# Where the two halves of each split operand lie in SBUF: tensor homes on 512-byte steps, and high and low half of a held operand side by side

## What is computed

```python
for layer in range(2):
    h = rms_norm(x, g_mix[layer])
    qkv = h @ w_in[layer]                    # 1024 x 3072
    ...                                      # attention gives mix
    x = x + mix @ w_out[layer]               # 1024 x 1024
    h2 = rms_norm(x, g_ffn[layer])
    u = h2 @ w_up[layer]                     # 1024 x 5632, then the convolution
    gate, val = jnp.split(u, 2, axis=-1)
    x = x + (jax.nn.silu(gate) * val) @ w_down[layer]   # 2816 x 1024
...                                          # second block: branches, w_out_2
q = h @ peer_wq                              # 1024 x 2048
hid = gelu(h @ peer_u.T)                     # 1024 x 16384, all experts
x = x + (gates * hid) @ peer_v               # 16384 x 1024
```

## Time and profile before

| | |
|---|---|
| median of 3 runs | 1750.53 us (1750.17 to 1751.01) |
| the profiled execution, its span | 1747.2 us |
| around the span, median less span | 3.3 us |
| TensorE busy, weight loads | 1691.7 us (97%), 1454.8 us (83%) |
| VectorE, ScalarE, GpSimd busy | 1149.2 us, 821.6 us, 706.5 us |
| HBM traffic | 279.33 MB read, 161 GB/s over the span |

### The profile page before, as it was taken

How to read it: one execution, slowest core, us unless ns; L and a number is a source line. 1 busy time by engine, 2 the same in 40 slices (tenths; PEclk the granted TensorE clock), 3 DMA queues, 4 the chain that set the end, 5 groups by cost and what they waited for, 6 DMA issues and landing times.

```text
span 1747.2 us, 27224 instructions
## 1 busy us (share of the span) xinstructions
PE 1691.7 (97%) x10714; PEld 1454.8 (83%) x10714; DVE 1149.2 (66%) x2422; ACT 821.6 (47%) x1453; POOL 706.5 (40%) x384
## 2 busy tenths in 40 slices
PE   7999999999999998999999999999999999999997
PEld 6779998777799986544579999999999988888885
DVE  6655785756367576666332999999999644444443
ACT  5455665354476642113243554544444455555553
POOL 2424667132357721432163999700000144444443
PEclk9999999999999999999999999999999999999998
DMA  7333545463255564323353656544444566666664
GB/s 292 112 109 132 182 162 195 150 217 108 74 193 190 173 203 134 111 87 109 95 194 134 216 167 198 179 147 145 145 140 139 160 193 193 194 194 195 195 193 134
DMA packets 77455, 283.20 MB, mean 162 GB/s; under 512 B 8720, under 2 KB 8976, under 8 KB 77072
## 3 DMA queue, kind: packets, MB, share of 16 engines
q1 hardware_dynamic: 76032, 276.50, 48.8%
q10 hardware_dynamic: 1296, 4.97, 0.8%
HBM read 279.33 MB, written 2.10 MB: 161 GB/s over the span
## 4 chain that ended last, share of the span: by engine, by line
PE 78%; DVE 8%; ACT 5%; POOL 5%; issue 3%; DMA 1%; POOLq 0%; DVEq 0%; ACTq 0%
PE bank L542 62%; PE bank L533 7%; PE bank L597 5%; POOL wl L2117 4%; ACT wh L1112 2%; DVE att L1478 2%; PE bank L665 1%; DVE wl L1461 1%; ACT att L1115 1%; PE bank L967 1%; PE bank L889 1%; DVE ssb L1467 1%; DVE mix L1506 1%; DVE xs L1467 1%; PE bank L837 0%
## 5 line engine op out<-in xcount | busy, mean ns | idle before, releaser
L2117 POOL TENSOR_TENSOR wl<-raw,wh 128x1024 fp32r<-128x1024 f32 x213 | 548.0, 2584 | 699.6 <-ACT wh L1112 691.1
L542 PE MATMUL bank<-hh,wh 128*128 128x256 f32 x1856 | 526.2, 284 | 5.5 <-POOL wl L2117 4.8
L1112 ACT ACTIVATE wh<-raw 128x1024 fp32r<-128x1024 f32 x476 | 492.7, 1050 | 57.2 <-PE bank L542 40.8
L542 PE MATMUL bank<-hl,wh 128*128 128x256 f32 x1856 | 519.1, 280 | 0.0
L542 PE MATMUL bank<-hh,wl 128*128 128x256 f32 x1856 | 518.1, 279 | 0.0
L1461 DVE TENSOR_TENSOR wl<-raw,wh 128x1024 fp32r<-128x1024 f32 x263 | 352.8, 1347 | 98.7 <-ACT wh L1112 98.2
L542 PEld LDWEIGHTS bank<-hh,wh 128*128 128x128 f32 x1856 | 349.1, 188 | 7.0 <-POOL wl L2117 6.0
L542 PEld LDWEIGHTS bank<-hl,wh 128*128 128x128 f32 x1856 | 349.2, 188 | 0.0
L542 PEld LDWEIGHTS bank<-hh,wl 128*128 128x128 f32 x1856 | 349.0, 188 | 0.0
L1467 DVE TENSOR_TENSOR acl<-H,ach 128x256 fp32r<-128x256 f32 x128 | 87.5, 685 | 181.6 <-ACT ach L1115 181.6
L542 PE MATMUL bank<-wh,ach 128*128 128x512 f32 x512 | 199.3, 389 | 0.4 <-DVE acl L1467 0.4
(11 more groups left out here) (216 smaller groups left out, 2313.4 us busy)
## 6 DMA issues: line engine op xcount, KB each, us to landing
raw<-in_ut_dram SPq DMA_DIRECT2D x128, 512.0 KB, 3.5
raw<-in_vt_dram SPq DMA_DIRECT2D x128, 512.0 KB, 3.8
raw<-in_wup_dram SPq DMA_DIRECT2D x88, 512.0 KB, 4.2
raw<-in_win_dram SPq DMA_DIRECT2D x48, 512.0 KB, 4.6
raw<-in_wdown_dram SPq DMA_DIRECT2D x44, 512.0 KB, 4.2
raw<-in_wout_dram SPq DMA_DIRECT2D x24, 512.0 KB, 3.6
raw<-in_wga_dram SPq DMA_DIRECT2D x16, 512.0 KB, 3.6
raw<-in_wpq_dram SPq DMA_DIRECT2D x16, 512.0 KB, 5.1
```

What stands on the lines that cost most here:

```text
L542: m = p.e.matmul(out, lhs[i][a], rhs[i][b], start=start and i == 0 and j == 0, stop=stop and i == n - 1 and j == 2)
L1112: a.e.activation(high_of(u), raw_of(u), ACTF.Copy).then_inc(act_hi.up(("hi", u)), 1)
L2117: g.e.tensor_tensor(low_of(u), raw_of(u), high_of(u).bitcast(F32), ALU.subtract).then_inc(pool_lo.up(("lo", u)), 1)
```

## The change

All tensors get sizes that are multiples of 128 floats (512 bytes) and `pad0` in front of them sets the first of them on such a step, so that every operand starts at a multiple of 512 bytes (a scratch of the DMA queues that the kernel does not use is made smaller to make room). High and low half of one operand now share one tensor. Where the operand is **held** by TensorE, each element's high half and low half lie side by side, so a half is read with a step of two floats (8 bytes): weights of `wup`, `wpq`, `ut` (`turned_units`), the activations `hT_held`, `y2`, `ac2`. Where it **moves**, the high half and then the low half lie as two contiguous blocks, as before. The engines that write a half, and those that read it to make the low half, do so with the same step. The number, order, shapes and engines of all instructions stay, and so do all waits.

```diff
+        scoped(ctx, "pad0", 96)
         xs = scoped(ctx, "xs", 2048)
...
-        hh, hl = scoped(sc_h, "hh", 2048, F32R), scoped(sc_h, "hl", 2048, F32R)
+        h2 = scoped(sc_h, "h2", 4096, F32R)
...
-        sta = scoped(ctx, "sta", 760)
+        sta = scoped(ctx, "sta", 768)
         raws = [scoped(ctx, f"raw{i}", 1024) for i in range(4)]
-        whs = [scoped(ctx, f"wh{i}", 1024, F32R) for i in range(4)]
-        wls = [scoped(ctx, f"wl{i}", 1024, F32R) for i in range(4)]
+        w2s = [scoped(ctx, f"w{i}", 2048, F32R) for i in range(4)]
...
-        con_s = scoped(early, "con", K_W - 128)
-        sml_s = scoped(early, "sml", S_W)
+        con_s = scoped(early, "con", 1664)
+        sml_s = scoped(early, "sml", 896)
...
-        yTh, yTl = [scoped(sc_f, f"y{c}", NTILE * 256, F32R)[:, :].rearrange("p (k t) -> p k t", k=NTILE) for c in "hl"]
+        y2 = scoped(sc_f, "y2", 2 * NTILE * 256, F32R)[:, :].rearrange("p (k t a) -> p a k t", k=NTILE, a=2)
+        yTh, yTl = y2[:, 0], y2[:, 1]
...
-        ach = [scoped(ctx, f"ach{j}", 256, F32R)[:, :] for j in range(2)]
-        acl = [scoped(ctx, f"acl{j}", 256, F32R)[:, :] for j in range(2)]
+        ac2 = [scoped(ctx, f"ac{j}", 512, F32R)[:, :].rearrange("p (t a) -> p a t", a=2) for j in range(2)]
+        ach, acl = [a[:, 0] for a in ac2], [a[:, 1] for a in ac2]
...
+        turned_units = set(itertools.chain(*[range(first["wup", L], first["wup", L] + 2 * NTILE) for L in range(DEPTH)],
+                                           range(first["wpq"], first["wpq"] + 16), range(first["ut"], first["ut"] + 128)))
+
+        def halves(i):
+            return w2s[slot[i]][:, :].rearrange("p (c a) -> p a c", a=2) if i in turned_units else w2s[slot[i]][:, :].rearrange("p (a c) -> p a c", a=2)
+
         def high_of(i):
-            return whs[slot[i]][:, 0:plan[i][1]]
+            return halves(i)[:, 0, 0:plan[i][1]]
 
         def low_of(i):
-            return wls[slot[i]][:, 0:plan[i][1]]
+            return halves(i)[:, 1, 0:plan[i][1]]
...
-        hTh = hh[:, :].rearrange("p (k t) -> p k t", k=8)
-        hTl = hl[:, :].rearrange("p (k t) -> p k t", k=8)
+        hT_moving = h2[:, :].rearrange("p (a k t) -> p a k t", a=2, k=8)
+        hT_held = h2[:, :].rearrange("p (k t a) -> p a k t", k=8, a=2)
...
+        def halves_for(st):
+            return hT_moving if st[0] == "f" else hT_held
...
-    nc = _bacc.Bacc("TRN2", target_bir_lowering=False, num_devices=1)
+    nc = _bacc.Bacc("TRN2", target_bir_lowering=False, num_devices=1, dynamic_dma_scratch_size=1024)
```

More of the change, by code:

```diff
@@ L1 @@
+import itertools
 import math
@@ L106, in program @@
         sc_h = ExitStack()
-        hh, hl = scoped(sc_h, "hh", 2048, F32R), scoped(sc_h, "hl", 2048, F32R)
+        h2 = scoped(sc_h, "h2", 4096, F32R)
         sc_h.close()
         hw, sel_s = scoped(ctx, "hw", 2048), scoped(ctx, "sel_s", 2048)
-        sta = scoped(ctx, "sta", 760)
+        sta = scoped(ctx, "sta", 768)
         raws = [scoped(ctx, f"raw{i}", 1024) for i in range(4)]
-        whs = [scoped(ctx, f"wh{i}", 1024, F32R) for i in range(4)]
-        wls = [scoped(ctx, f"wl{i}", 1024, F32R) for i in range(4)]
+        w2s = [scoped(ctx, f"w{i}", 2048, F32R) for i in range(4)]
         early = ExitStack()
-        con_s = scoped(early, "con", K_W - 128)
-        sml_s = scoped(early, "sml", S_W)
+        con_s = scoped(early, "con", 1664)
+        sml_s = scoped(early, "sml", 896)
         tab_s = scoped(early, "tab", 8192)
         raws += [scoped(early, f"raw{i}", 1024) for i in (4, 5)]
-        whs += [scoped(early, f"wh{i}", 1024, F32R) for i in (4, 5)]
-        wls += [scoped(early, f"wl{i}", 1024, F32R) for i in (4, 5)]
+        w2s += [scoped(early, f"w{i}", 2048, F32R) for i in (4, 5)]
         sc_l = ExitStack()
@@ L303, in sml, with hT @@
             return sml_s[:, c:c + n]
-        def hT(k, cols):
-            return hTh[:, k, cols], hTl[:, k, cols]
+        def halves_for(st):
+            return hT_moving if st[0] == "f" else hT_held
+        def hT(k, cols, of=hT_held):
+            return of[:, 0, k, cols], of[:, 1, k, cols]
         iota = con(K_IOTA, 128)
@@ L436, in program @@
         H = H_s[:, :].rearrange("p (j t) -> p j t", j=128)
-        R_AT = 16800
-        assert R_AT >= K_W - 128 + S_W + 8192 + 6144
+        R_AT = 16896
+        assert R_AT >= 1664 + 896 + 8192 + 6144
         r_at = [R_AT]
@@ L616, in by_features @@
                             m = mm3(banks[b][:, 0:256], [unit_pair(i, k, kt, tcols(c)) for k in range(kt)],
-                                    [hT(off + k, ALLC) for k in range(kt)], True, True, ready)
+                                    [hT(off + k, ALLC, hT_moving) for k in range(kt)], True, True, ready)
                         else:
@@ L798, in pe @@
                         m = mm3(banks[b][:, 256 * half:256 * half + 256], [unit_pair(i, k, 8, tcols(0)) for k in range(8)],
-                                [hT(k, ALLC) for k in range(8)], True, True, ready_both(("f", L)))
+                                [hT(k, ALLC, hT_moving) for k in range(8)], True, True, ready_both(("f", L)))
                         m.then_inc(pe_out.up(("used", i), ("up", L, f, half)), 1)
@@ L1040, in hidden @@
                 claim(b)
-                m = mm3(banks[b][:, 0:256], [unit_pair(i, k, 8, tcols(0)) for k in range(8)], [hT(k, ALLC) for k in range(8)], True, True, ready_both(("f", 2)))
+                m = mm3(banks[b][:, 0:256], [unit_pair(i, k, 8, tcols(0)) for k in range(8)], [hT(k, ALLC, hT_moving) for k in range(8)], True, True, ready_both(("f", 2)))
                 m.then_inc(pe_out.up(("used", i), ("hid", j)), 1)
@@ L1141, in turned @@
                         a.wait_ge(pe_out, ("T", st, t, k))
-                        do(hTh[:, k:k + n, tcols(t)], quad(ps("T", st, t, k), n), ACTF.Copy, ("hTh", st, t, k))
+                        do(halves_for(st)[:, 0, k:k + n, tcols(t)], quad(ps("T", st, t, k), n), ACTF.Copy, ("hTh", st, t, k))
             def exps(tag, maps, buf, i):
@@ L1163, in act @@
             stream_up_to(first["win", 0])
-            load(con_s[:, :], consts_d[:, 128:K_W], con_in, "con")
+            load(con_s[:, 0:K_W - 128], consts_d[:, 128:K_W], con_in, "con")
             load(sml(0, S_W), smalls_d, sml_in, "sml")
@@ L1178, in out_turned @@
                     a.wait_ge(pe_out, ("mT", L, g))
-                    do(hTh[:, 2 * g:2 * g + 2, :], ps("mT", L, g)[:, :].rearrange("p (k t) -> p k t", k=2), ACTF.Copy, ("mTh", L, g))
+                    do(hT_held[:, 0, 2 * g:2 * g + 2, :], ps("mT", L, g)[:, :].rearrange("p (k t) -> p k t", k=2), ACTF.Copy, ("mTh", L, g))
                 def att_step(c):
@@ L1507, in scale, with halves_low @@
                                              ).then_inc(dve_out.up(("nrm", st, t, q), ("used", row) if t and q else None), 1)
-            def halves_low(k0, n, cols, src, hi, ev):
+            def halves_low(of, k0, n, cols, src, hi, ev):
                 v.wait_ge(act_out, hi)
-                tt(hTl[:, k0:k0 + n, cols], src, hTh[:, k0:k0 + n, cols].bitcast(F32), ALU.subtract, ev, alone=True)
+                tt(of[:, 1, k0:k0 + n, cols], src, of[:, 0, k0:k0 + n, cols].bitcast(F32), ALU.subtract, ev, alone=True)
             def turned(st, ts_, nq, q0=0):
@@ L1515, in turned @@
                     for k, n in parts(st, q0, nq):
-                        halves_low(k, n, tcols(t), quad(ps("T", st, t, k), n), ("hTh", st, t, k), ("hT", st, t, k))
+                        halves_low(halves_for(st), k, n, tcols(t), quad(ps("T", st, t, k), n), ("hTh", st, t, k), ("hT", st, t, k))
             def reduced(out, src, tmp, quarter, ev):
@@ L1735, in out_turned @@
                 def out_turned(g):
-                    halves_low(2 * g, 2, ALLC, ps("mT", L, g)[:, :].rearrange("p (k t) -> p k t", k=2), ("mTh", L, g), ("mT", L, g))
+                    halves_low(hT_held, 2 * g, 2, ALLC, ps("mT", L, g)[:, :].rearrange("p (k t) -> p k t", k=2), ("mTh", L, g), ("mT", L, g))
                 def added(t, n):
```

## The result

The change makes the kernel slower: 1775.77 us (median of 4 runs, 1773.75 to 1778.14) against 1750.57 us beside it, a ratio of 1.0147 with a 95% interval of 1.0134 to 1.0160. The forecast was 1687.5 us, the range 1668 to 1745: wrong in size and in sign. The profiled execution took 1778.14 us with a span of 1776.3, against a span of 1747.2 before, so 29.1 us have to be found.

What follows compares the result with a forecast made beforehand. TensorE's `mm3` matmuls were taken to bound the kernel. Gains of 12.7 + 2.5 + 10.9 + 16.7 + 8.4 + 11.8 = 63.0 us took the span from 1747.2 to 1684.2, the median to 1687.5; range 1668 to 1745.

Steps and rivals of the forecast that it cites:

- What bounds the kernel: Opening step: `mm3`'s matmuls on TensorE, busy 97% of the span, set the end, so their start-to-start cost decides.
- What the layout does to the meeting: Step on TensorE's weight load and moving stream: interleaved held halves make both advance 8 bytes and keep their distance.
- the floors: Lowest start-to-start times assumed for TensorE's fp32r matmuls: about 112 ns for 256 columns, 216 ns for 512.
- The yardstick: Plain fp32 matmuls on TensorE, only 2.7 ns over their column time, taken as the measure for fp32r matmuls.
- excess: Matmul time above the lowest assumed: 4.7 ns in `ut`, 6.0 `wup`, 6.5 `wpq`, 10.9 `vt`, about 16 `wdown`, 17 `win`.
- The homes: Operand start addresses on 512-byte steps; as a rival, expected to bring matmuls to 116.7 and 226.8 ns.
- Rows 5: Profile rows of two `wdown` units, same code, different addresses: 226.7 against 233.3 ns a matmul, read as addresses costing time.
- only the homes work: Rival for all `mm3` stages: the step changes nothing, addresses give the best values seen; 10.8 us gained, 1740; chance 0.09.
- the load gets slower: Rival on TensorE's stepped held load: excess doubled, 69 us more, 1820; chance 0.14 together with GpSimd beyond its limit.
- no change: Rival on TensorE: its read ports are independent, so addresses cost nothing and the time stays 1750.5; chance 0.04.
- The other engines: Step pricing stepped reads and writes of halves on VectorE, ScalarE and GpSimd at nothing, GpSimd's cover being thin.
- What takes something back in `ut`: Term for `ut`: GpSimd's two passages lose 1.5 us and VectorE's last rounds 2, leaving 10.9 of 14.4 us.

Runs made afterwards that it cites:

- e8: The changed kernel with all halves contiguous, 512-byte start addresses kept and the moving activations `hT_moving` shifted by 48 floats: 1742.42 us, ratio 0.9954.
- e2: The changed kernel with all halves in contiguous blocks, so only the start addresses on 512-byte steps remain: 1755.84 us, ratio 1.0037.
- e6: The changed kernel with the old sizes of `pad0`, `sta`, `con` and `sml`, so the step stays without the 512-byte start addresses: 1776.64 us, ratio 1.0154.
- e4: The changed kernel with held activations in contiguous blocks; held weights keep their step, start addresses stay on 512-byte steps: 1758.33 us, ratio 1.0050.
- e5: Separate kernel, TensorE alone: segments of matmuls in the kernel's address order, moving operand shifted 0 to 60 floats, several held steps; 256 columns, step 1, shift 0: 120.0 ns.
- e9: Separate kernel, TensorE alone: 512 columns at step 1 over shifts of the moving operand, then 256 columns; 512 columns took 228.9 to 236.7 ns at fifteen nonzero shifts.
- e7: The changed kernel with all halves contiguous, 512-byte start addresses kept and the moving activations `hT_moving` shifted by 8 floats: 1745.28 us, ratio 0.9971.
- e1: Separate kernel: TensorE alone with the held operand's step and shift varied, then elementwise instructions with and without a step; 256 columns, step 1, unshifted: 120.0 ns.

## Why the prediction was wrong

- **What bounds the kernel** held for what the change did: `mm3`'s distance from start to start sets the end, and all else of size follows from it. It would not have held for the gain in early `ut`, as e8 shows (below).
- **"What the layout does to the meeting"** is the step that failed: "With the held halves interleaved, the load also passes 8 bytes: both advance alike and keep their distance", so that the floors would be met. Two things stand in its place. A load with a step of two floats has a floor of its own, 117.8 ns instead of 111.6, so the 112 taken for 256 columns could not be reached; and the extra time did not vanish: 120.0 ns in all slots for 256 columns, 233.3 to 235.6 for 512, where contiguous halves at an equal phase have 226.7. What in the chip makes load and stream hinder each other was not measured; that the distance depends on shift and step with nothing but TensorE at work was.
- **The yardstick** The earlier trace rows did not carry over. Its 2.7 ns were read rightly but belong to fp32 matmuls, which take twice as long for the same bytes. No mean of an fp32r segment or stage of 512 columns in any run is under 226.7 ns, against the 216 of the forecast, and for 256 the least is 113.3, against 112. Of `ut`'s excess of 4.7 ns 3.4 were a matter of addresses, as assumed; of `vt`'s 10.9, nothing that these runs could remove.
- **The homes** were taken as neutral or better, because the earlier trace rows show equal phase as the better one. That is right for 512 columns (`wdown` at 226.8 to 227.1 in all slots in e2) and wrong for 256, where it is the worse: 116.7 to 120.0 in `ut`. Rows 5 are 512-column rows, and the rival "only the homes work" gave all products the best value seen, 116.7 for 256 columns. It forecast -10.8 us; e2 against before is +6.4.
- **The rival that came true** is "the load gets slower". Its condition (256-column products over 117 ns) was met at 120.0, though the homes alone meet it too (e2), so that this sign could not tell the two apart and e6 had to; its price, the excess doubled (+69 us), was too high, as the excess of 256 columns went from 4.7 to 8.0 and that of `vt` from 10.9 to 19.5 while `win` hardly moved. Its chance of 0.14 was too low: nothing measured stood behind a held operand with a step, and the text said so itself, yet took the favourable end.
- **The rule of the Trainium skill** (SBUF — State Buffer, "Who interferes with whom": the two read ports of TensorE are independent, and it never waits on anyone) would have said no change. Fifteen shifts of one 512-column segment from 226.9 to 236.7 ns speak against it once more, so rejecting it was right; what it was rejected for was only half understood.
- **The other engines.** VectorE at nothing: right, 1225 and 1226 ns. ScalarE at nothing: 60 ns short (1056 to 1116 alone, 1050 to 1095 on average in the kernel), with no effect seen, as it is under its cover. GpSimd at nothing: 2338 to 2388 alone, 2%, and 2584 to 2622 in the kernel. The Trainium skill (GPSIMD Engine Reference, "Performance pitfalls for Q7 kernels") has its cliff only over 8 bytes, and the trace agrees. Its cover is gone in the two passages of the chain, and these are 1.1 us longer in e4 than in e2.
- **What takes something back in `ut`** named GpSimd's passages and the last rounds, and priced the first at 1.5 us. It left out VectorE's routing, which has 0.5 us of reserve before: in e8 all 4.4 us of early `ut` are gone, and the floors of the forecast would have met the same limit.

## What to carry to other kernels

When TensorE is what bounds the kernel, count starts in a window before and after: here a busy share of 97% hides between 113 and 120 ns for one and the same matmul. The phase of the moving operand against the held one is a knob worth a sweep in a small kernel, for each width on its own: 256 columns and 512 had opposite answers at phase 0. Look too for the next chain behind it: here VectorE's routing stood 0.5 us behind TensorE, and no row of busy shares shows that. A step of 2 in the held operand is not free, and a layout argued from a neighbouring data type should first be timed by itself, in the segment that it is meant for.

## What the runs showed of the hardware

- The start-to-start distance of contiguous fp32r matmuls of 256 columns lies between 113.3 and 123.3 ns, of 512 columns between 226.7 and 236.7, with nothing but the shift between the two operands changed (e5, e9). Shifts that differ by 64 floats gave the same: 48 and 112 both 113.3; for the held operand 0 and 64 both 120.0, with 512 columns both 226.7, once the first starts are left out.
- At one shift there can be two steady distances: 113.3 and 117.8 ns at 48 floats, 116.7 and 117.8 at 8, and with a step of 2 and 512 columns 233.3 and 235.5 at 0. In `wup` of e7 and e8 and in `wdown` of the changed kernel the value changes behind a distance of 147 to 349 ns. What picks it stays open.
- A moving fp32r operand with a step of two floats takes about 230 ns for 256 columns at a clock of 1.00, with a contiguous held operand or one with a step (e1): nearly twice the contiguous 120. A held one with that step costs 6% of the load at the 2.4 GHz level and nothing at the 1.2 GHz level (213.3 ns with either), with a step of four twice the load at 2.4 GHz.
